# Two FFN layers of a Trainium2 kernel: one contiguous mixed operand, and two of four weight-block sums made by an accumulating DMA

## The reference

```python
h = rmsnorm(x, norm_ffn[i])
x = x + (jax.nn.silu(h @ w_gate[i]) * (h @ w_up[i])) @ w_down[i]
```

## Time and profile before

| | |
|---|---|
| median of 3 runs | 1581.62 us (1581.22 to 1581.68) |
| the profiled execution | 1581.13 us |
| its span, first to last instruction | 1579.3 us |
| mean granted TensorE clock | 0.999 |
| PE busy | 1571.0 us |
| DVE, ACT, POOL busy | 1067.9, 723.0, 130.5 us |
| products of layer 0 | 263.9 to 424.6 us |
| products of layer 1 | 769.9 to 930.4 us |

### The profile page before, as it was taken

The page is one execution under the profiler, slowest core; times in us unless marked ns, Lnnn a source line. Parts: engine busy times, 40 slices in busy tenths (PEclk is TensorE's granted clock), DMA queues, the critical chain, the costliest instruction groups (busy, mean ns, idle before and its releaser), DMA issues.

```text
span 1579.3 us, 23274 instructions
## 1 busy us (share of the span) xinstructions
PE 1571.0 (99%) x8492; PEld 1309.2 (83%) x8492; DVE 1067.9 (68%) x1583; ACT 723.0 (46%) x1270; POOL 130.5 (8%) x121
## 2 busy tenths in 40 slices
PE   9999999999999999999999999999999999999998
PEld 7877888999988876778899988887777778888887
DVE  7666678888833366767888885438667657556566
ACT  6333345666722345554566663322455542233334
POOL 2000200000010100030000001114111111000000
PEclk9999999999999999999999999999999999999999
DMA  6422333333323341133333355343121121333344
GB/s 226 147 80 81 101 99 106 103 106 104 126 92 102 68 109 47 39 102 107 104 100 105 105 182 211 127 177 119 54 68 54 41 61 41 87 106 93 95 128 152
DMA packets 48941, 164.07 MB, mean 104 GB/s; under 512 B 6011, under 2 KB 9308, under 8 KB 48476
## 3 DMA queue, kind: packets, MB, share of 16 engines
q1 hardware_dynamic: 44752, 152.46, 31.2%
q10 hardware_dynamic: 4108, 10.52, 2.0%
HBM read 156.38 MB, written 6.59 MB: 103 GB/s over the span
## 4 chain that ended last, share of the span: by engine, by line
PE 97%; DVE 2%; issue 0%; ACT 0%; POOL 0%; DVEq 0%; POOLq 0%; ACTq 0%
PE ps L2497 21%; PE ps L2499 20%; PE ps L2498 20%; PE ps L2720 5%; PE ps L2719 5%; PE ps L2718 5%; PE ps L2726 4%; PE ps L2728 2%; PE ps L3036 1%; PE ps L3058 1%; PE ps L3024 1%; PE ps L2833 1%; PE ps L2866 1%; PE ps L3164 1%; PE ps L3163 1%; PE ps L3162 1%
## 5 line engine op out<-in xcount | busy, mean ns | idle before, releaser
L1478 DVE TENSOR_TENSOR w_lo<-raw,w_hi 128x1024 fp32r<-128x1024 f32 (+4 forms) x184 | 242.6, 1318 | 129.1 <-ACT w_hi L853 128.4
L853 ACT ACTIVATE w_hi<-raw 128x1024 fp32r<-128x1024 f32 (+4 forms) x184 | 193.6, 1052 | 295.2 <-PE ps L2499 269.6
L2497 PE MATMUL ps<-a_hi,w_hi 128*128 128x512 f32 x632 | 255.6, 404 | 0.7 <-DVE t L1513 0.4
L2499 PE MATMUL ps<-a_hi,w_lo 128*128 128x512 f32 x632 | 246.8, 391 | 0.0
L2498 PE MATMUL ps<-a_lo,w_hi 128*128 128x512 f32 x632 | 246.4, 390 | 0.0
L2497 PEld LDWEIGHTS ps<-a_hi,w_hi 128*128 128x128 f32 x632 | 118.7, 188 | 32.5 <-issue 7.8
L2499 PEld LDWEIGHTS ps<-a_hi,w_lo 128*128 128x128 f32 x632 | 118.6, 188 | 25.9
L2498 PEld LDWEIGHTS ps<-a_lo,w_hi 128*128 128x128 f32 x632 | 118.9, 188 | 22.0
L2497 PE MATMUL ps<-g_hi_b,w_hi 128*128 128x512 f32 x246 | 95.7, 389 | 0.0
L2498 PE MATMUL ps<-g_lo_b,w_hi 128*128 128x512 f32 x246 | 95.7, 389 | 0.0
L2499 PE MATMUL ps<-g_hi_b,w_lo 128*128 128x512 f32 x246 | 95.7, 389 | 0.0
(11 more groups left out here) (463 smaller groups left out, 3737.8 us busy)
## 6 DMA issues: line engine op xcount, KB each, us to landing
raw<-w SPq DMA_DIRECT2D x134, 512.0 KB, 3.6
raw<-w8b SPq DMA_DIRECT2D x62, 512.0 KB, 3.6
raw<-w_down SPq DMA_DIRECT2D x32, 704.0 KB, 4.1
w<-cmp_w SPq DMA_DIRECT2D x2, 2048.0 KB, 11.2
raw<-block_spill SPq DMA_DIRECT2D x8, 512.0 KB, 4.7
raw<-w_blocks SPq DMA_DIRECT2D x6, 512.0 KB, 4.4
raw<-w_out_first SPq DMA_DIRECT2D x8, 320.0 KB, 2.8
even_row<-w_last ACTq DMA_DIRECT2D x4, 512.0 KB, 5.4
```

The source lines that it names most:

```text
L853: act.activation(w_hi[:, slot, 0:w], raw[:, raw_slot, 0:w], ACT.Copy)\
L1478: dve.tensor_tensor(w_lo[:, slot, 0:w], raw[:, raw_slot, 0:w], w_hi[:, slot, 0:w].bitcast(F32), ALU.subtract).then_inc(w_lo_ready, 1)
L2497: pe.matmul(o, wh, a_h, start=start and at == 0, stop=False)
L2499: ins = pe.matmul(o, wl, a_h, start=False, stop=stop and at == kt - 1)
```

## The change

It has three parts. (1) mixed_both is laid out so that the high and the low part of one operand stand side by side; the 512-column matmul of a wide product reads 512 elements in a run, and writes one run. The number and shape of matmuls are the same. (2) The slots of a pair are addressed as one (raw_pair): SP loads gate0, up0, up0 (w_three, 768 KB) and up1, gate1 (w_two, 512 KB), both when all low parts of the pair two before are written, and POOL then issues a DMA that adds gate0 and up1 (w_added, 512 KB) onto the two copies of up0. So up0+gate0 and up0+up1 lie in raw, and DVE makes only the other two sums, in sums_w. (3) The two ready sums (first_t) are rounded first of all for a pair, ahead of b11; the other two (last_t) are split between product3, which took its operand from the first two, and product5. For the first pair of a layer first_t_high waits for the last mixed operand to be written, and last_t_high stands ahead of b22_high. Semaphores of another stage (cmp_hidden, cmp_turned, cmp_mm) become one that is counted up; its waits are the same.

```diff
-    mixed_both = at("mixed_both", [P, 2, 4, KT // 2, HS], R32, a_at)
-    mixed_hi, mixed_lo = mixed_both[:, 0], mixed_both[:, 1]
-    sums_w = at("sums_w", [P, 6, S], F32, tmp_at)
+    mixed_both = at("mixed_both", [P, 4, KT // 2, 2, HS], R32, a_at)
+    mixed_hi, mixed_lo = mixed_both[:, :, :, 0, :], mixed_both[:, :, :, 1, :]
+    sums_w = at("sums_w", [P, 2, S], F32, tmp_at)
...
+            def load_pairs(layer, b):
+                with sp.Fori(0, PRODS // 2, 1) as i:
+                    for j in range(2):
+                        n = i * RAW + (b + 2 * j)
+                        sp.wait_ge(w_lo_ready, n - 2)
+                        sp.dma_start(raw_pair[:, j, 0:3 * S], a["w_three"][i * 2 + (PRODS * layer + j)])\
+                            .then_inc(raw_in[2 * j], 16)
+                        sp.wait_ge(w_lo_ready, n - 2)
+                        sp.dma_start(raw_pair[:, j, 3 * S:5 * S], a["w_two"][i * 2 + (PRODS * layer + j)])\
+                            .then_inc(raw_in[2 * j + 1], 16)
...
+            def pair_sums(layer, b):
+
+                for p in range(PRODS):
+                    j = p % 2
+                    pool.wait_ge(raw_in[2 * j], 16 * ((b + 2 * p) // RAW + 1))
+                    pool.dma_start(raw_pair[:, j, S:3 * S], a["w_added"][PRODS * layer + p], accum_op=ALU.add)\
+                        .then_inc(pair_sum[j], 16)
+
+            squares(V_FFN0)
+            power(V_FFN0)
+            pair_sums(0, N_FFN0 + 2 * PLAIN)
+            squares(V_MIX1)
+            power(V_MIX1)
...
                     rounded(m)
+                first_t_high(layer, n0, 0, 0)
                 b11_high(layer, n0, 0, 0)
                 gate(PLAIN - 1)
-                t12_high(layer, n0, 0, 0)
+                last_t_high(layer, n0, 0, 0)
                 b22_high(layer, n0, 0, 0)
-                t43_high(layer, n0, 0, 0)
...
-            def t12_high(layer, n0, i, j):
-                act.wait_ge(sums_ready, i * 6 + (SUMS * layer + 3 * KT + 3 * j + 2))
+            def first_t_high(layer, n0, i, j):
+                b = n0 + 2 * PLAIN
+                act.wait_ge(pair_sum[j], i * 16 + (PRODS // 2 * layer + 1) * 16)
-                    act.wait_ge(prod_done, i * 10 + (5 * PRODS * layer + 5 * j - 7))
+                    act.wait_ge(blk_done, i * 4 + (b + 2 * j - 3))
                 elif j:
-                    act.wait_ge(blk_done, n0 + 2 * PLAIN)
-                act.activation(t12_hi[j][:], sums_w[:, 0:2, :], ACT.Copy).then_inc(t_hi_ready, 1)
+                    act.wait_ge(blk_done, b)
+                else:
+                    act.wait_ge(sums_ready, SUMS * layer + 3 * KT)
+                act.activation(first_t_hi[j][:].rearrange("p t s -> p (t s)"), raw_pair[:, j, S:3 * S], ACT.Copy)\
+                    .then_inc(t_hi_ready, 1)
 
             def b22_high(layer, n0, i, j):
...
                         seeded_c(layer, i, j)
+                        first_t_high(layer, n0, i1, j1)
                         b11_high(layer, n0, i1, j1)
                         gate_first(layer, qb, i, j)
-                        t12_high(layer, n0, i1, j1)
                         b22_high(layer, n0, i1, j1)
                         seeded_d(layer, b, i, j)
                         held(b, i, j)
-                        t43_high(layer, n0, i1, j1)
+                        last_t_high(layer, n0, i1, j1)
...
-                sums_first(layer, n0, 0, 0)
+                first_t_low(layer, 0, 0)
                 b11_low(n0, 0, 0)
-                sums_last(layer, 0, 0)
-                t12_low(layer, 0, 0)
+                sums_last(layer, n0, 0, 0)
                 scaled(n0 + 2 * m + 1, plain_bank(m, 1), tmp[:, 2 * (m % 2) + 1, :])
+                last_t_low(layer, 0, 0)
                 b22_low(n0, 0, 0)
                 gated(m)
-                t43_low(layer, 0, 0)
                 products(layer, n0, q0 + 2 * PLAIN)
 
...
+                dve.wait_ge(pair_sum[j], i * 16 + (PRODS // 2 * layer + 1) * 16)
+                dve.wait_ge(raw_in[2 * j + 1], i * 16 + (b // RAW + 1) * 16)
+                dve.tensor_tensor(sums_w[:, 0, :], raw_pair[:, j, S:2 * S], raw_pair[:, j, 3 * S:4 * S], ALU.add)\
                     .then_inc(sums_ready, 1)
-                dve.wait_ge(sums_ready, i * 6 + (SUMS * layer + 3 * KT + 3 * j + 1))
-                dve.tensor_tensor(sums_w[:, 1, :], sums_w[:, 0, :], raw[:, 2 * j + 1, 0:S], ALU.add)\
+                dve.wait_ge(sums_ready, i * 4 + (SUMS * layer + 3 * KT + 2 * j + 1))
+                dve.tensor_tensor(sums_w[:, 1, :], sums_w[:, 0, :], raw_pair[:, j, 4 * S:5 * S], ALU.add)\
...
-                        sums_first(layer, n0, i1, j1)
+                        sums_last(layer, n0, i1, j1)
+                        first_t_low(layer, i1, j1)
                         b11_low(n0, i1, j1)
-                        sums_last(layer, i1, j1)
-                        t12_low(layer, i1, j1)
                         b22_low(n0, i1, j1)
                         negative_up(layer, i, j)
-                        t43_low(layer, i1, j1)
+                        last_t_low(layer, i1, j1)
                         gate_up(layer, qb, i, j)
...
-                    pe.matmul(ps[:, bank, :].rearrange("p (h s) -> p h s", h=2), wh, mixed_both[:, :, t, k, :],
+                    pe.matmul(ps[:, bank, :], wh, mixed_both[:, t, k].rearrange("p h s -> p (h s)"),
...
-                product((t12_hi[j][:, 1], t12_lo[j][:, 1]), mixed_half(2), ps[:, j, 0:HS]).then_inc(prod_done, 1)
+                pe.wait_ge(t_lo_ready, i * 4 + (2 * PRODS * layer + 2 * j + 2))
+                product((last_t_hi[j][:, 0], last_t_lo[j][:, 0]), mixed_half(2), ps[:, j, 0:HS]).then_inc(prod_done, 1)
...
-                pe.wait_ge(t_lo_ready, i * 4 + (2 * PRODS * layer + 2 * j + 2))
-                product((t43_hi[j][:, 1], t43_lo[j][:, 1]), mixed_half(0), ps[:, j, HS:S]).then_inc(blk_done, 1)
+                product((first_t_hi[j][:, 1], first_t_lo[j][:, 1]), mixed_half(0), ps[:, j, HS:S]).then_inc(blk_done, 1)
 
             def product5(layer, i, j):
                 pe.wait_ge(seeded, i * 10 + (5 * PRODS * layer + 5 * j + 4))
-                product((t43_hi[j][:, 0], t43_lo[j][:, 0]), plain_half(2), ps[:, 3, 0:HS]).then_inc(blk_done, 1)
+                product((last_t_hi[j][:, 1], last_t_lo[j][:, 1]), plain_half(2), ps[:, 3, 0:HS]).then_inc(blk_done, 1)
 
...
+        "w_three": beside(gate0, up0, up0),
+        "w_two": beside(up1, gate1),
+        "w_added": beside(gate0, up1),
```

More of the change, by code:

```diff
@@ L392, in build @@
     seeded = sem("seeded")
+    pair_sum = [sem(f"pair_sum{j}") for j in range(2)]
     up_high = sem("up_high")
@@ L669, in _ @@
             for n in range(N_QM1, N_OUT1):
-                load(n, n % RAW, a["w8"][n - N_QM1 + N_DOWN0], KT * P)
+                load(n, n % RAW, a["w8"][n - N_QM1 + N_FFN0 + 2 * PLAIN], KT * P)
                 if n == N_QM1 + 3:
@@ L681, in _ @@
                 load(N_OUT2 + m, m % RAW, a["w_out_late"][m], late_width(N_OUT2))
-            with sp.Fori(0, (N_DOWN1 - N_FFN1) // RAW, 1) as i:
+            with sp.Fori(0, 2 * PLAIN // RAW, 1) as i:
                 for j in range(RAW):
-                    load(i * RAW + (N_FFN1 + j), j, a["w8"][i * RAW + (N_DOWN0 + N_OUT1 - N_QM1 + j)], KT * P)
+                    load(i * RAW + (N_FFN1 + j), j, a["w8"][i * RAW + (N_FFN0 + 2 * PLAIN + N_OUT1 - N_QM1 + j)],
+                         KT * P)
+            load_pairs(1, N_FFN1 + 2 * PLAIN)
             with sp.Fori(0, 2 * KT // RAW, 1) as i:
@@ L1064, in b22_high, with last_t_high @@
                     act.wait_ge(blk_done, b - 1)
-                act.activation(b22_hi[:].rearrange("p t s -> p (t s)"), raw[:, 2 * j + 1, 0:2 * S], ACT.Copy)\
+                act.activation(b22_hi[:].rearrange("p t s -> p (t s)"), raw_pair[:, j, 3 * S:5 * S], ACT.Copy)\
                     .then_inc(w_hi_ready, 1)
-            def t43_high(layer, n0, i, j):
+            def last_t_high(layer, n0, i, j):
                 b = n0 + 2 * PLAIN
-                act.wait_ge(sums_ready, i * 6 + (SUMS * layer + 3 * KT + 3 * j + 3))
+                act.wait_ge(sums_ready, i * 4 + (SUMS * layer + 3 * KT + 2 * j + 2))
                 if not isinstance(i, int) or i:
@@ L1074, in t43_high @@
                     act.wait_ge(blk_done, b)
[L1075 removed]
+                act.activation(last_t_hi[j][:], sums_w[:], ACT.Copy).then_inc(t_hi_ready, 1)
             def seeded_b(layer, qb, i, j):
@@ L1787, in mixed_low, with sums_last @@
                     .then_inc(sums_ready, 1)
-            def sums_first(layer, n0, i, j):
+            def sums_last(layer, n0, i, j):
                 b = n0 + 2 * PLAIN
@@ L1806, in b11_low, with first_t_low @@
                     .then_inc(w_lo_ready, 1)
[L1808 to L1813 removed]
+            def first_t_low(layer, i, j):
                 dve.wait_ge(t_hi_ready, i * 4 + (ROUNDED * layer + KT + 2 * j + 1))
[L1815 removed]
```

(24 more changed lines are left out.)

48 lines of the change are left out of this document (18 added, 30 removed).

## The result

| | before | changed |
|---|---|---|
| median | 1581.62 us (1580.93 to 1581.76, 9 runs) | 1587.93 us (1580.98 to 1594.14, 9 runs) |
| ratio | | 1.0042, 95% interval 1.0029 to 1.0056 |
| profiled execution, its span | 1581.13, 1579.3 us | 1594.14, 1592.3 us |

The change made the kernel slower by 0.42%, where I had forecast 1580.8 us and no change that can be told. The time also lost its steadiness: nine runs of before lie within 0.8 us, nine of the changed kernel at 1581.0, 1584.5, five times 1587.2 to 1588.3, and 1593.5 and 1594.1. The profiled execution is one of the slowest, 13.0 us longer in its span, so it shows everything that can go wrong at once. One run of the kernel before beside the experiments (1699.56 us, granted clock 0.863) was in a slower state and is compared with nothing.

The account below looks back on a forecast made before the run. PE was taken to bound the kernel; -1.5 us for the contiguous operand and +0.7 for the entry, others 0, sum to -0.8, giving 1580.8 us; likeliest range 1579.5 to 1582, 8 in 10 from 1578.0 to 1592.

Parts of the forecast that it names:

- What bounds the kernel: Whole kernel: PE is busy 1571.0 of 1579.3 us, so only shorter PE steps or PE waits change the time.
- Contiguous operand of the wide product: FFN products: 512-column matmuls reading one run instead of two pieces get faster, 1.5 us gained, bounds 0 and 2.1.
- rival (e): Wide products: the layout gives nothing and only the cost at the stage's entry remains, 1582.3 us; chance 0.10.
- Entry of the stage: Start of each layer's products: new order makes product 7 of pair 0 and product 1 of pair 1 late, +0.7 us.
- Steady order: Middle of the products stage: reordered sums and roundings still arrive in time, slack 0.45 and 0.4 us, cost 0.
- rival (c): Steady products: b11_low or last_t_low slightly late in every pair; at 0.6 instead of 0.4, 6 us, 1587; chance 0.05.
- Rival (b): Products stage: POOL can issue transfers only when DVE pauses, +75 to +150 us; chance 0.03.
- Rival (d): Products: 128x256 matmul steps beyond the wide products also speed up, 117.5 instead of 120 ns, 4.8 us more, 1576; chance 0.06.
- Sums moved to the DMA, in the steady state: Products: DVE saves 39 us, worth 0 to PE; a 7 us accumulating transfer is hidden with 3.6 us to spare.
- Sums moved to the DMA, the tightest place: Pair 2 of each layer: load 4.3 us, transfer 7 against 6.9 of room, 0.4 us slack before PE, no cost.
- It hurts from 7.3 us on, us for us: Pair 2, both layers: each us of accumulating transfer beyond 7.3 us costs PE one us.
- Rival (a): Accumulating transfers slow: +3.2 us at 9.3, +15 or +42 at 11.2; chance 0.08 for 7.3 to 9.3, 0.12 beyond.

Follow-up runs that it names:

- e1: The kernel before with only mixed_both's layout changed, high and low operand side by side; 1581.35 us, ratio 1.0000.
- e2: The changed kernel with SP holding pair 3's loads back until product 6 of pair 1 is done; 1581.57 us, ratio 1.0001.
- e3: The changed kernel with POOL's accumulating transfers as plain copies of the same bytes, addition left out; 1582.18 us, ratio 1.0007.
- e5b: The changed kernel with pair 2's loads held back until pair 0's products reach their sixth; 1593.89 us, ratio 1.0081.
- e7b: The changed kernel with the high b22 ahead of last_t_high at the stage's entry, on ACT alone; 1586.98 us, ratio 1.0031.
- e4: The changed kernel with b22 of pair 0 moved earlier at the stage's entry on both ACT and DVE; 1581.39 us, ratio 1.0005.
- changed again: The changed kernel, unaltered, run a second time beside the kernel before; 1582.56 us, ratio 1.0011.
- e6b: The kernel of e4 with each accumulating transfer done twice, one behind the other; 1673.55 us, ratio 1.0592.

## Why the prediction was wrong

**What bounds the kernel:** right. PE is the bound, and what was lost in the two stages was lost where PE rested, came late or ran at the lower clock.

**Contiguous operand of the wide product (-1.5):** wrong, it is 0. The 7 ns between 396 and 389 are lengths of overlapping rows, and the 226.7 ns are strips of 512-column matmuls only; neither is a price of the layout, as e1 shows. The Trainium skill (SBUF — State Buffer, Door 1: The DMA port swizzle) gave 0 here, and the measurement sides with it: 235 ns in both layouts. It was my rival (e).

**Entry of the stage (+0.7):** right in kind, half in size. Ahead of product 1 of pair 1 PE loses 0.16 us a layer, 0.3 in all, where I had 0.33 a layer; so it is in each of the six traces with DVE's new order at the entry (the changed kernel twice, e2, e3, e5b, e7b), and not in e4. Product 7 of pair 0 is not late.

**Steady order (0) and its rival (c):** right, as the windows from 300 and 806 us on show. **Rival (b)** is dead too: POOL's issue of 0.87 us at 274.79 runs while DVE is busy from 274.77 to 276.19. **Rival (d)** did not happen: matmuls of 256 columns in the products are 120 ns from start to start before and after.

**Sums moved to the DMA, in the steady state:** right. The turn of ACT came 14.9 us after the load (351.2 to 366.1), and 4.2 + 5.7 leave 5 us. What DVE saves is 33.3 us of busy time (1067.9 to 1034.6), where I had 39; neither is worth anything to PE.

**Sums moved to the DMA, the tightest place:** this is the step that failed. The place, the chain and the room were right: 11.1 us from the load of pair 2 to ACT's turn (268.99 to 280.13), where I had 11.2, and 0.6 us of slack at PE, where I had 0.4. The sizes in it were wrong. I put 4.3 us for the load and 7 for the transfer, each priced alone and neither dependent on the other's neighbours. Pair 2 fourteen times, in seven executions (the changed kernel twice):

| kernel, layer | load of pair 2 | pair 3's load behind POOL's issue | transfer | PE waits | clock behind |
|---|---|---|---|---|---|
| e4, 0 | 4.8 | 5.22 | 5.5 | 0 | full |
| e4, 1 | 5.0 | 5.02 | 6.0 | 0 | full |
| e2, 1 | 5.8 | 2.30 | 5.3 | 0 | full |
| e2, 0 | 6.4 | 1.70 | 5.8 | 0.30 | full |
| changed again, 0 | 4.8 | 1.17 | 5.7 | 0 | full |
| changed again, 1 | 5.3 | 0.67 | 7.6 | 1.20 | full |
| e7b, 0 | 5.4 | 0.64 | 7.7 | 1.35 | full |
| e7b, 1 | 5.6 | 0.34 | 9.1 | 3.03 | half |
| changed, 0 | 5.8 | 0.20 | 8.9 | 2.96 | half |
| changed, 1 | 5.8 | 0.14 | 9.1 | 3.20 | half |
| e5b, 0 | 4.4 | -2.01 | 7.4 | 3.58 | half, for 3.41 us |
| e5b, 1 | 4.3 | -1.91 | 7.6 | 3.61 | half |
| e3 (copy), 0 | 5.2 | 0.82 | 3.8 | 0 | full |
| e3 (copy), 1 | 5.6 | 0.38 | 4.6 | 0 | full |

With the load of pair 3 issued 1.17 us or more behind POOL's, the accumulating transfer takes 5.3 to 6.0 us. With that load 0.67 us behind it or less, or ahead of it, it takes 7.4 to 9.1. No others take as long: of the 192 accumulating transfers in the six executions without e3 and e6b the other 185 take 5.2 to 6.9. And the load of pair 2 decides which it is: the two loads are 6.0 us apart, because DVE writes the low b22 of pair 1 only 6 us behind that of pair 0. So a load of 4.8 us leaves 1.2 and all is well; a load of 5.8 leaves 0.2 and the transfer is 3 us longer too. One microsecond of luck in a load becomes 4 in the sum, which is why the times of the changed kernel scatter as they do. That this is the cause is shown from both sides: keep pair 3's load away (e2) or load pair 2 earlier (e4), and the wait is gone; let both loads come together (e5b), and it is there, by the times in each run. A plain copy in the same place (e3) does not make PE wait either, for its shorter packets or for its earlier start.

A rule of the Trainium skill would have raised the question: DMA: Bandwidth & Descriptors (Queues, rings and completion order) says that a DMA engine drains a whole packet, of many descriptors, from one queue before it turns to the next. The trace agrees as far as it goes: the transfer's data begins at 278.92, when the three blocks of the load issued behind it (275.96 to 279.48) are nearly through.

**"It hurts from 7.3 us on, us for us":** the second failure. With PE's waits of 2.96 us and more comes a stretch of 6.83 us at the lower clock, which begins 2.0 to 2.4 us after PE has come to rest and costs another 2.6 to 3.0 us (in one layer of e5b it begins 1.3 us behind the wait, is 3.41 us long and costs 1.8). With those of 0.3 to 1.35 it does not come; they cost 0.25 us more than their length. The low clock is 5.9 of the 13.0 us in the profiled execution, and no term of the sum had it.

**Rival (a)** was the nearest, "a slow transfer hurts first at pair 2", and had the right sign and place. It asked how slow a transfer is, as one number for all 32, and so got 0.12 where it decides; by its formula the measured 9.1 us gives +3, where both layers together lost 12 there.

What stays open: why the load of pair 2 takes 4.8 us in one execution and 5.8 in the next, how the runs share out between the cases (two sets of runs gave medians 5.4 us apart), and what in the accumulating transfer, its packets or its late start, makes it lose to the load.
